# Conv-in and both query projections with high and low activations side by side in one 512-column matmul

## The reference, cut to what matters

```python
# layer 0: gated short convolution, w_in is 1024 x 3072
b_gate, c_gate, v = split(rmsnorm(x, mix_norm[0]) @ w_in, 3)
y = (b_gate * causal_conv3(c_gate * v)) @ w_out
# both layers: cross attention, w_q is 1024 x 1024
q = (rmsnorm(x, xa_norm[i]) @ w_q).reshape(seq, 4, 256)
s = einsum("bshd,bmhd->bhsm", q, k) * 256 ** -0.5
```

## Time and profile before

| | |
|---|---|
| median of three runs | 1319.8 us |
| the profiled execution | 1319.97 us |
| its span | 1318.2 us |
| mean granted TensorE clock | 0.99 |
| TensorE matmul busy | 98% of the span |
| VectorE busy | 76% |
| ScalarE busy | 58% |
| GpSimd busy | 18% |
| TensorE on the chain that ended last | 83% |
| VectorE on it | 8% |

### The profile page before, as it was taken

The page is one execution under the profiler, slowest core; times in us unless marked ns, Lnnn a source line. Parts: engine busy times, 40 slices in busy tenths (PEclk is TensorE's granted clock), DMA queues, the critical chain, the costliest instruction groups (busy, mean ns, idle before and its releaser), DMA issues.

```text
span 1318.2 us, 24123 instructions
## 1 busy us (share of the span) xinstructions
PE 1291.9 (98%) x8348; PEld 1178.8 (89%) x8348; DVE 1000.5 (76%) x1541; ACT 762.0 (58%) x1375; POOL 237.7 (18%) x324
## 2 busy tenths in 40 slices
PE   7999999999999999999999999999999999999997
PEld 6888889989997888888888888999989998888886
DVE  5788777678668888777888668998967767888854
ACT  6555544356556655555556447778855655655642
POOL 2233110112001111111111101024451201111111
PEclk9999999999999999999999999999989999999999
DMA  6656645545444656645556645444445544555660
GB/s 211 214 191 193 218 163 173 180 159 176 145 130 158 195 188 201 220 154 172 192 185 218 199 153 178 158 155 130 129 128 193 176 145 130 183 185 188 224 202 36
DMA packets 60551, 228.32 MB, mean 173 GB/s; under 512 B 6848, under 2 KB 7360, under 8 KB 60352
## 3 DMA queue, kind: packets, MB, share of 16 engines
q1 hardware_dynamic: 60048, 226.60, 52.9%
q10 hardware_dynamic: 432, 0.79, 0.2%
HBM read 226.31 MB, written 1.05 MB: 172 GB/s over the span
## 4 chain that ended last, share of the span: by engine, by line
PE 83%; DVE 8%; ACT 4%; issue 2%; POOL 1%; DMA 0%; DVEq 0%; ACTq 0%; SPq 0%; POOLq 0%
PE bank L1263 83%; DVE w_lo L741 3%; ACT w_hi L374 2%; DVE acc L744 2%; DVE acc L741 1%; DVE x L741 1%; ACT sq L407 1%; ACT corr L374 1%; DVE t L741 0%; DVE h L744 0%; DMA x<-x_t 0%; PE bank L1412 0%; DVE m L741 0%; ACT xd L374 0%; DVE a L744 0%
## 5 line engine op out<-in xcount | busy, mean ns | idle before, releaser
L741 DVE TENSOR_TENSOR w_lo<-raw,w_hi 128x1024 fp32r<-128x1024 f32 (+2 forms) x403 | 521.4, 1297 | 38.8 <-ACT w_hi L374 37.0
L1263 PE MATMUL bank<-h,w_hi 128*128 128x512 f32 (+1 forms) x2056 | 480.3, 362 | 11.9 <-DVE h L744 6.8
L374 ACT ACTIVATE w_hi<-raw 128x1024 fp32r<-128x1024 f32 (+2 forms) x403 | 442.6, 1099 | 52.1 <-PE bank L1263 51.4
L1263 PEld LDWEIGHTS bank<-h,w_hi 128*128 128x128 f32 x2056 | 357.4, 192 | 60.8 <-DVE h L744 8.6
L1263 PE MATMUL bank<-a,w_hi 128*128 128x512 f32 (+1 forms) x1664 | 365.0, 344 | 1.0 <-POOL a L1185 0.7
L1263 PEld LDWEIGHTS bank<-a,w_hi 128*128 128x128 f32 x1664 | 283.3, 191 | 32.2 <-POOL a L1185 1.1
L1263 PE MATMUL bank<-h,w_lo 128*128 128x256 f32 x1736 | 291.1, 283 | 0.0
L1263 PEld LDWEIGHTS bank<-h,w_lo 128*128 128x128 f32 x1736 | 257.6, 192 | 14.6
L374 ACT ACTIVATE corr<-bank 128x256 f32<-128x256 f32 x233 | 88.6, 381 | 266.7 <-PE bank L1263 266.7
L1263 PE MATMUL bank<-a,w_lo 128*128 128x256 f32 x1280 | 230.8, 283 | 0.0
L1263 PEld LDWEIGHTS bank<-a,w_lo 128*128 128x128 f32 x1280 | 193.6, 191 | 7.2
(11 more groups left out here) (184 smaller groups left out, 1135.8 us busy)
## 6 DMA issues: line engine op xcount, KB each, us to landing
raw<-w_gu SPq DMA_DIRECT2D x174, 512.0 KB, 3.5
raw<-w_down SPq DMA_DIRECT2D x64, 704.0 KB, 4.1
raw<-w_xbc SPq DMA_DIRECT2D x32, 512.0 KB, 3.6
raw<-w_conv_in SPq DMA_DIRECT2D x24, 512.0 KB, 3.6
raw<-w_q SPq DMA_DIRECT2D x16, 512.0 KB, 4.0
raw<-w_k SPq DMA_DIRECT2D x16, 512.0 KB, 3.6
raw<-w_v SPq DMA_DIRECT2D x16, 512.0 KB, 3.5
raw<-w_o SPq DMA_DIRECT2D x16, 512.0 KB, 3.7
```

The lines of the kernel that those rows point to most:

```text
L374: return nc.scalar.activation(out, in_, ACT.Copy, scale=scale)
L741: return nc.vector.tensor_tensor(out, a, b, op)
L1263: return nc.tensor.matmul(out, lhs, rhs, start=start, stop=stop, skip_group_check=check)
```

## The change

Conv_in, q0 and q1 go over from `unit` to `pair_unit`. ScalarE gets a `corr_copy` for each of their 40 tiles, VectorE a sum (`joined`), and what it multiplied straight out of the bank it now multiplies from SBUF in a second instruction, after a wait for the sum. A semaphore `scaled_ready` tells ScalarE that the scaled tile is there, where `evac` did.

```diff
+            def joined(phase, t, out):
+                b, use = bank_use(phase, t)
+                dve.wait_ge(corr_ready, pair_first[phase] + t + 1)
+                tt(out, bank[b][:, 0:SEQ], corr[t % 2][:, :], ALU.add).then_inc(evac[b], 1)
@@ VectorE, conv() @@
                     if t == 0:
                         norm(NORM_MIX0)
+                        joined("conv_in", 0, t1[0][:, :])
                         split(n0 + 1 + AHEAD)
-                    dve.wait_ge(unit_done, n0 + t + 1)
                     if q == 0:
-                        tt(t1[0][:, :], bank[b][:, 0:SEQ], rms_k[:, :]).then_inc(evac[b], 1)
                         if t:
+                            joined("conv_in", t, t1[0][:, :])
                             split(n0 + t + AHEAD)
                         dve.wait_ge(evac[b], use + 1)
+                        step(tt(t1[0][:, :], t1[0][:, :], rms_k[:, :]))
                     elif q == 1:
-                        tt(padded[:, 2:2 + SEQ], bank[b][:, 0:SEQ], t1[0][:, :]).then_inc(evac[b], 1)
+                        joined("conv_in", t, gate[0][:, :])
                         ...
+                        step(tt(padded[:, 2:2 + SEQ], gate[0][:, :], t1[0][:, :]))
                     else:
-                        tt(t2[j % 2][:, :], bank[b][:, 0:SEQ], acc[0][:, :]).then_inc(evac[b], 1)
+                        joined("conv_in", t, t2[j % 2][:, :])
+                        dve.wait_ge(evac[b], use + 1)
+                        tt(t2[j % 2][:, :], t2[j % 2][:, :], acc[0][:, :]).then_inc(scaled_ready, 1)
                         split(n0 + t + AHEAD)
@@ ScalarE, conv() @@
                     split(n0 + t + AHEAD)
                     if t == 1:
                         norm(NORM_MIX0)
+                    if t > 1:
+                        b, use = bank_use("conv_in", t - 2)
+                        act.wait_ge(evac[b], use + 1)
+                    corr_copy(t % 4, t, n0 + t)
                     if t % 3 == 2:
-                        act.wait_ge(evac[b], use + 1)
+                        act.wait_ge(scaled_ready, CONV_SCALED + t // 3 + 1)
                         copy(a_hi[:, t // 3, :], t2[t // 3 % 2][:, :]).then_inc(ahi_ready, 1)
@@ ScalarE, attention(): corr_copy(0, 0, n0) at s == 0 ahead of split(n0 + 1 + AHEAD), and @@
                         if s + 2 < KT:
                             new_mem(layer, s + 2)
-                        b, use = bank_use(f"q{layer}", s)
-                        act.wait_ge(evac[b], use + 1)
+                        if s:
+                            corr_copy(s % 4, s, n0 + s)
+                        act.wait_ge(scaled_ready, Q_SCALED[layer] + s + 1)
                         copy(a_hi[:, KT + s, :], t2[s % 2][:, :]).then_inc(ahi_ready, 1)
@@ VectorE, attention(): q_sum(layer, 0) behind norm(...), and @@
+            def q_sum(layer, t):
+                at_least(dve, a_ready, Q_A[layer] + t - 1)
+                joined(f"q{layer}", t, t2[t % 2][:, :])
                         b, use = bank_use(f"q{layer}", s)
-                        tt(t2[s % 2][:, :], bank[b][:, 0:SEQ], rms_k[:, :]).then_inc(evac[b], 1)
+                        if s:
+                            q_sum(layer, s)
+                        dve.wait_ge(evac[b], use + 1)
+                        tt(t2[s % 2][:, :], t2[s % 2][:, :], rms_k[:, :]).then_inc(scaled_ready, 1)
                         if s > 1:
                             split(n0 + s + AHEAD)
@@ TensorE, project() @@
-                opening(unit, name, b)
+                opening(pair_unit, name, b)
                 for t in range(4, tiles):
-                    unit(first[name] + t, free(name, t), KT, 0, h, True, True)
+                    pair_unit(first[name] + t, free(name, t), KT, 0, h, True, True)
```

More of the change, by code:

```diff
@@ L214, in trunk @@
         kv_hi, k_ready = sem("kv_hi"), sem("k_ready")
+        scaled_ready = sem("scaled_ready")
         s_done, max_ready, exp_ready, probs_ready = sem("s_done"), sem("max_ready"), sem("exp_ready"), sem("probs_ready")
@@ L252, in trunk @@
         FFN_A = {0: 0, 1: FT + KT + KT, 2: 2 * FT + 2 * KT, 3: 3 * FT + 3 * KT}
+        CONV_SCALED, Q_SCALED = 0, {0: KT, 1: 2 * KT}
         CONV_A, Q_A = FT, {0: FT + KT, 1: 3 * FT + 2 * KT}
@@ L257, in trunk @@
         for name, units, _ in PHASES:
-            if name in X_COUNT or name[:2] == "gu":
+            if name in X_COUNT or name[:2] == "gu" or name in ("conv_in", "q0", "q1"):
                 pair_first[name] = pair_count
@@ L494, in conv @@
                         norm(NORM_MIX0)
+                    if t > 1:
+                        b, use = bank_use("conv_in", t - 2)
+                        act.wait_ge(evac[b], use + 1)
+                    corr_copy(t % 4, t, n0 + t)
                     if t % 3 == 2:
-                        b, use = bank_use("conv_in", t)
-                        act.wait_ge(evac[b], use + 1)
+                        act.wait_ge(scaled_ready, CONV_SCALED + t // 3 + 1)
                         copy(a_hi[:, t // 3, :], t2[t // 3 % 2][:, :]).then_inc(ahi_ready, 1)
@@ L509, in attention @@
                         new_mem(layer, 1)
+                        corr_copy(0, 0, n0)
                         split(n0 + 1 + AHEAD)
@@ L923, in attention @@
                         norm(2 if layer == 0 else 6)
+                        q_sum(layer, 0)
                         split(n0 + 1 + AHEAD)
@@ L931, in attention @@
                     if s < KT:
-                        dve.wait_ge(unit_done, n0 + s + 1)
                         b, use = bank_use(f"q{layer}", s)
-                        at_least(dve, a_ready, Q_A[layer] + s - 1)
-                        tt(t2[s % 2][:, :], bank[b][:, 0:SEQ], rms_k[:, :]).then_inc(evac[b], 1)
+                        if s:
+                            q_sum(layer, s)
+                        dve.wait_ge(evac[b], use + 1)
+                        tt(t2[s % 2][:, :], t2[s % 2][:, :], rms_k[:, :]).then_inc(scaled_ready, 1)
                         if s > 1:
@@ L1392, in ffn, with project @@
                     pair(i, None)
-            def project(name, b, tiles=KT, extra=None):
-                opening(unit, name, b)
+            def project(name, b, tiles=KT):
+                opening(pair_unit, name, b)
                 for t in range(4, tiles):
-                    unit(first[name] + t, free(name, t), KT, 0, h, True, True)
+                    pair_unit(first[name] + t, free(name, t), KT, 0, h, True, True)
             def scores(h):
```

## The result

The changed kernel takes 1328.5 us in the median of five runs (1324.8 to 1330.6), against 1319.8 before; the ratio is 1.0059, 95% interval 1.0043 to 1.0076. So it is slower by 0.6%, where 1323.4 was forecast, and outside the range's end of 1326.8. The profiled execution took 1324.8 us (span 1323.0).

A forecast was written before the change was run, and what follows sets the result against it. PE was taken as the bound in conv_in, q0 and q1, with DVE and ACT as cover. From 1319.97 us, -0.48 (conv_in) + 2.36 (q0) + 1.53 (q1) gave 1323.4 us; range 1319.3 to 1326.8.

The forecast's parts named there:

- TensorE per unit: Conv_in, q0, q1: a pair unit takes 2.79 instead of 2.88 us on PE, -3.6 us over 40 units.
- Conv_in: Whole conv_in phase: of 2.1 us of TensorE time saved about 0.5 are left, -0.48 us.
- the way from there to the last activation tile: Conv_in's tail: added copy, product and second product step for tiles 22 and 23 lengthen the path by 1.32 us.
- The hold-up near the opening: Start of conv_in: DVE splits unit 5 later than PE wants it, +0.27 us (ends 0 and +0.6).
- q0's opening: Start of q0: w_lo matmuls deferred behind the wait for h(k), +0.65 us; unit 2 gives 0.09 back.
- q's ring: q0 and q1, units 5 to 8: copy, sum, product and rounding wait in turn on ACT and DVE, +1.8 us each.
- The first turn: q0, before unit 5: PE gets unit 5 6.61 instead of 5.06 us after the product of tile 0.
- the ring takes 2.58, and PE is ahead again: q from unit 9 on: no memory tile in the step, so a turn takes 2.58 us and PE leads.
- rival B: New PE idle behind conv_in and at unit 5 brings half-clock stretches, 1.5 us each; two give 1326.4 us; chance 0.25.
- Rival A: PE bound throughout, no ring because DVE and ACT have idle time: 1318.7 us, not slower; chance 0.13.
- C's missing stretch at 302: The half-clock stretch at 302 us, at q0's opening, disappears: 1321.9 us; chance 0.14.
- D: Conv_in, q0, q1: a pair unit is no cheaper than the old one, 1325.5 us; chance 0.06.

The follow-up runs named there:

- after_fill: Changed kernel with unused matmuls in its new or longer PE idle times (behind conv_in, q0's opening, before unit 5 of q0 and q1); 1327.1 us, ratio 1.0052.
- q_only: Changed kernel with conv_in back in its old form, so only q0 and q1 use the pair form; 1327.3 us, ratio 1.0046.
- before_fill: Kernel before, with unused matmuls added in the openings of q0, gate/up 1 and gate/up 3 and in the SSD; 1320.2 us, ratio 0.9998.
- copy_first: Changed kernel with ScalarE's copy moved ahead of its weight and memory splits in steps 1 to 7 of q; 1320.7 us, ratio 1.0014.
- after_open: Changed kernel with every opening's first unit cut into blocks 0 to 5, 6 and 7, so w_lo matmuls run before the wait for tile 6; 1323.2 us.

## Why the prediction was wrong

**TensorE per unit, right.** 2.79 to 2.80 us a unit of the pair form, as forecast, so 0.09 saved. In the changed kernel 512 columns take 0.230 us from start to start and 256 columns 0.120, so each of the 8 blocks saves 2 x 0.120 - 0.230 = 0.01. The prediction set 0.02 a unit against this, by a formula of the Trainium skill ("TensorE: Matmul & The Clock Gate", section "Back-to-back issue gap"). That section gives the formula for an isolated matmul, and says that in a stream of weight loads and matmuls both set the distance. Every matmul here has a weight load of its own, and the trace has 0.230 where the formula gives 0.216.

**Conv_in: right in mechanism, a little too much expected.** `after_fill` and `q_only` differ by conv_in alone and have no stretch from norm to norm: 97.18 and 97.13, +0.05; with -0.26 ahead of the norm that is -0.21, where -0.48 was forecast. PE starts unit 23 1.63 us sooner than before, not 1.80, and the way from there to the last activation tile grew by 1.40, not 1.32 (the sum at 269.18 is 0.48 behind the copy's start, not 0.40). The hold-up near the opening is there, 0.27 before unit 5 and 0.08 before unit 6. That the forecast of 0.27 fits so well is luck: the figures given for it (0.73 + 4.87 against 2 x 2.79) make 0.02, and the terms listed for the 4.87 make 4.84.

**q0's opening, about right.** `q_only` 97.13 against 96.73 for `before_fill`, both without a stretch: +0.40, where 0.65 - 0.09 was forecast.

**q's ring: the right step, the wrong sum. This is what failed.** 1.8 us a q was forecast, 3.1 measured. The first turn: PE got unit 5 6.86 us after the first product, not 6.61; the next three turns took 3.05, 3.10 and 3.01, not 2.98, as the sum starts 0.46 and not 0.39 behind a copy for which DVE is already waiting, and unit 5 starts 1.36 and not 1.26 behind the start of its split. That gives k0 16.02 us behind the first product instead of 13.77 before: 2.25. Another 0.1 is ahead of the first product. The rest, 0.75, lies between k0 and the probabilities, where the prediction says that from unit 9 on "the ring takes 2.58, and PE is ahead again". That step is false. DVE's backlog of splits reached `k_lo`, and the scores waited (0.45 us at 336.35; their first matmul comes 9.32 us behind k0, against 8.64 before). I had followed DVE only to where its weight splits were early again, and not to its next consumer. `copy_first` shows that all 3.1 belong to this one order. (The step of 2.35 us before is 2.37 by the prediction's own sum and 2.34 in the trace; nothing hangs on it.)

**The clock: rival B came in part, and its price was too high.** At equal clock the parts sum to -0.26 (from the memory's norm to conv_in's, 55.51 against 55.77) + 0.45 (from there to q0) + 3.1 (q0) - 0.23 (SSD norm to q1's norm, 231.30 against 231.53 with two stretches each) + 3.06 (q1) = +6.1 us, where the forecast had 3.4; the means differ by 7.5. The other 1.4 go with the clock: its mean is 0.9891 over the 11 runs of the changed kernel and 0.9908 over 71 of the 76 of the kernel before, whose own runs take 1320.0 us at 0.990 and 1317.3 at 0.993, so about 0.9 a thousandth; that makes 1.5, an estimate. B had two new stretches of 1.5 us. The one behind conv_in always came, and cost 0.9. The idle 1.8 us before unit 5 was followed by a stretch in one of eight cases (q0 and q1 of both executions of the changed kernel, of `q_only` and of `after_open`), and that one cost next to nothing. Where the rest of the 1.4 falls is open. That B's sum of 1326.4 lies near the measured mean of 1327.3 is luck: 1.6 us too much for the clock against 2.7 too little for the ring and the other parts. With the 6.1 alone the mean would have been 1325.9, inside the range; it took both to leave it. The three runs ahead of the prediction lay within 3 us, the 76 lie within 5.9, and the range had little room for that: those 76 moved up by 6.1 reach from 1323.1 to 1329.0, and the 11 runs from 1324.8 to 1330.6.

Rival A (bound by PE throughout) is refuted by the 1.83 us idle. C's missing stretch at 302 happened in one profile of the changed kernel and not in the other. D is refuted by the 2.79.

## What to carry to other kernels

Where a busy engine's instructions are shortened by handing work to two engines that look idle, the order inside their streams decides and not their load: put the short instruction that others wait for (here a 0.36 us copy) ahead of the long prefetch work. Follow a backlog to the last consumer that it can reach, not to the first that is no longer late. And compare single profiles only part by part, with the half-clock stretches of each part beside it.

## What the runs showed of the hardware

A granted clock of 0.50 set in during or within 2 us of idle times of PE of about 2 us, in some executions and not in others of the same program: at the 2.2 us behind conv_in in five of five profiled executions, at the 1.9 to 2.6 us in the opening of q0 in four of eight, at the 2.2 us in those of gate/up 1 and gate/up 3 in four of eight each, at the 2.6 us in the SSD in twelve of thirteen, at the 1.7 to 1.8 us before unit 5 of q0 and q1 in one of eight. A stretch cost 1.3 to 1.6 us where PE is the bound, 0.9 in conv_out, and 0.1 at most in q0's ring, where it is not.

Matmuls whose result nobody uses, put exactly into these idle times, went with a full clock there: no stretch at q0 in six filled executions, none at gate/up 1 and 3 in five. Filled in the SSD too, the five runs lay within 1.7 us. Put 22 us of time away from the wait (989.8 against 967.9) they cost their own length, 2.0 us for nine, and the wait of 2.6 us stayed.
